# SiLU and tanh as single table functions in a fused two-block transformer kernel, with a shorter routing step

## What is computed

```python
# first block
c_act = silu(causal_conv(c, conv_w, conv_b))
h = head_layernorm(mlstm(...), m_norm_g) + m_skip * c_act
y_m = sigmoid(z) * h
y_d = rmsnorm(diff_attention(qd, kd, vd, lam, rel_bias), da_norm_g) * (1 - lam_init)
x = x + concat([y_m, y_d]) @ w_out
lg = h2 @ w_rg + b_rg                       # 4 groups; best group by top_k
le = (h2 @ w_re + b_re)[best group]         # 8 experts; best two by top_k
gates = one_hot(eid) * (pg_sel * softmax(top_v))
for e in range(32):                         # 32 experts, hidden 512
    hid = silu(t @ w_eg[e]) * (t @ w_eu[e])
    out = out + gates[:, e:e+1] * (hid @ w_ed[e])
# second block, two layers
x = x + 0.5 * rmsnorm((silu(a) * b) @ w_out)       # a, b = split(rmsnorm(x) @ w_in); width 2816
xbc = silu(causal_dwconv(xbc));  y_ssd = rmsnorm(ssd(xbc, dt) * silu(z))
y_ret = groupnorm(retention(q, k, v)) * silu(g)
y_att = sliding window attention with sinks
y = sum over branches of sigmoid(gate + b_gate) * (y_branch @ w_branch);  x = x + rmsnorm(y @ w_out)
x = x + 0.5 * rmsnorm(feed-forward again)
```

## Time and profile before

| what | before |
|---|---|
| median of 3 runs | 2215.17 us (2214.47 to 2215.31) |
| the profiled execution's own time | 2214.65 us |
| its span, first to last instruction | 2212.8 us |
| PE busy | 2024.2 us (91%) |
| DVE busy | 1154.8 us (52%) |
| ACT busy | 1096.2 us (50%) |
| mean granted clock of PE, of full speed | 0.937 |
| moved by DMA | 486 MB, 220 GB/s on average |

### The profile page before, as it was taken

One profiled execution on the slowest core, in us unless ns is written; L12 is line 12 of the kernel. 1 busy time (PEld: TensorE's weight loads), 2 busy tenths in 40 slices (PEclk: granted clock), 3 DMA queues, 4 the chain that ended last, 5 costly groups with the idle time before them and its releaser, 6 DMA issues.

```text
span 2212.8 us, 31344 instructions
## 1 busy us (share of the span) xinstructions
PE 2024.2 (91%) x13110; PEld 1639.5 (74%) x13110; DVE 1154.8 (52%) x1468; ACT 1096.2 (50%) x1368; POOL 50.2 (2%) x99
## 2 busy tenths in 40 slices
PE   8978677777789999999999999999999999999998
PEld 7863212111269978987799999899879888898997
DVE  5763111111146656647566565465575565655663
ACT  5520000000068934553555897498544635646992
POOL 0000000000000000000000000000000000001000
PEclk9988877777789999999999999999999999999999
DMA  6558999999974554432344555535545233354552
GB/s 270 212 225 334 421 421 421 421 421 421 421 304 151 213 189 173 170 114 96 114 172 172 191 177 188 181 134 229 190 171 189 97 115 123 127 189 174 181 182 94
DMA packets 66904, 486.14 MB, mean 220 GB/s; under 512 B 7424, under 2 KB 7424, under 8 KB 8544
## 3 DMA queue, kind: packets, MB, share of 16 engines
q1 hardware_dynamic: 65632, 476.25, 56.3%
q0 software_dynamic: 1152, 8.16, 1.0%
HBM read 483.33 MB, written 1.05 MB: 219 GB/s over the span
## 4 chain that ended last, share of the span: by engine, by line
PE 77%; DMA 10%; SPq 6%; DVE 3%; ACT 2%; issue 1%; POOL 1%; DVEq 0%; ACTq 0%; POOLq 0%
PE bank L1534 35%; PE bank L1621 11%; PE bank L456 10%; DMA work<-in_w_experts 9%; PE bank L1837 8%; SPq L1434 6%; PE bank L1548 3%; PE bank L1362 1%; PE bank L1392 1%; PE bank L1415 1%; PE bank L1078 1%; PE bank L2067 1%; ACT rows L2222 1%; PE bank L1937 1%; PE bank L1964 0%
## 5 line engine op out<-in xcount | busy, mean ns | idle before, releaser
L1534 PE MATMUL bank<-work_parts 128*128 128x256 f32 x2240 | 581.2, 283 | 0.0
L1512 DVE TENSOR_TENSOR ring_parts<-ring,work_parts 128x2048 fp32r<-128x2048 f32 x200 | 457.6, 2291 | 232.3 <-ACT work_parts L1505 219.7
L1505 ACT ACTIVATE work_parts<-ring 128x2048 fp32r<-128x2048 f32 x200 | 380.8, 1908 | 202.5 <-PE bank L1621 98.3
L1534 PE MATMUL bank<-columns_parts,work_parts 128*128 128x256 f32 x1472 | 417.9, 284 | 2.1 <-DVE rows_parts L680 1.9
L1534 PE MATMUL bank<-columns_parts,ring_parts 128*128 128x256 f32 x1472 | 416.8, 283 | 0.0
L1534 PEld LDWEIGHTS bank<-work_parts 128*128 128x128 f32 x2240 | 411.6, 192 | 0.1
L1534 PEld LDWEIGHTS bank<-columns_parts,work_parts 128*128 128x128 f32 x1472 | 282.8, 192 | 3.1 <-DVE ring_parts L669 2.3
L1534 PEld LDWEIGHTS bank<-columns_parts,ring_parts 128*128 128x128 f32 x1472 | 282.5, 192 | 0.0
L1621 PE MATMUL bank<-work_parts 128*128 128x512 f32 x704 | 217.3, 389 | 0.0
L1392 PE MATMUL bank<-work 128*32 128x512 f32 x640 | 126.7, 888 | 60.6 <-DMA work<-in_w_experts 60.6
L1534 PE MATMUL bank<-rows_parts,work_parts 128*128 128x256 f32 x640 | 181.7, 284 | 0.0
(11 more groups left out here) (388 smaller groups left out, 2776.4 us busy)
## 6 DMA issues: line engine op xcount, KB each, us to landing
ring<-in_w_layers SPq DMA_DIRECT2D x242, 1024.0 KB, 4.8
work<-in_w_experts SPq DMA_DIRECT2D x136, 1024.0 KB, 26.9
ring<-in_w_experts SPq DMA_DIRECT2D x48, 1024.0 KB, 26.7
ring<-in_w_first SPq DMA_DIRECT2D x16, 1024.0 KB, 4.9
columns<-in_w_experts SPq DMA_DIRECT2D x8, 1024.0 KB, 26.6
work<-in_post POOLq DMA_DIRECT2D x3, 1024.0 KB, 5.5
work<-in_second POOLq DMA_DIRECT2D x1, 2944.0 KB, 11.4
work<-in_first SPq DMA_DIRECT2D x1, 1805.5 KB, 11.2
```

The lines of the kernel that those rows point to most:

```text
L1505: act.activation(his[j % len(his)], m.ring[U.slot(names[j])], ACT.Copy).then_inc(F["unit_hi"], 1)
L1512: dve.tensor_tensor(m.ring_r[slot], m.ring[slot], his[j % len(his)].bitcast(F32), ALU.subtract).then_inc(F["unit_lo"], 1)
L1534: mm = pe.matmul(out, w, x, start=k + n == 0, stop=k == KT - 1 and n == 2)
```

## The change

It replaces Exp, Ln, Exp and a multiplication by one Silu wherever SiLU is wanted: the convolutions of both blocks, the experts' gate, the feed-forward, rg and z of the mixer. Where a sigmoid is wanted (the first block's gate, the branch gates), it uses sigmoid(x) = (1 + tanh(x/2)) / 2. ACT takes tanh from the bank, DVE does (t + 1) * y in one instruction, and the factor 1/2 goes into the step that makes the high and the low part. In the first block z.1 is projected before h is turned, and DVE does the normalisation of the attention half before the skip and the gate. The routing chain loses a few small operations: the two token halves go together, the subtraction of the two best logits moves behind `chosen`, and before the first selection only the first pass's ranks are made. SP's order of loads follows. The diff, cut:

```diff
-              + [f"vdtok.{t}" for t in range(2)] + ["z.0", "dout.0", "dout.1", "hT.0", "hT.1", "z.1", "ydT.0", "ydT.1"]
+              + [f"vdtok.{t}" for t in range(2)] + ["z.0", "dout.0", "dout.1", "z.1", "hT.0", "hT.1", "ydT.0", "ydT.1"]
...
@@ first_scalar
     act.wait_ge(*F.at("conv", 4))
-    step(act.activation(m.ec, m.cv, ACT.Exp, scale=-1.0))
-    sigmoid_tail(act, step, m.ec, F["conv_sig"])
+    act.activation(m.cv, m.cv, ACT.Silu).then_inc(F["cact"], 1)
...
-        act.activation(m.ez[:, 2 * i:2 * i + 2, :], split(ps[B.bank(job)][:], 2), ACT.Exp, scale=-1.0).then_inc(B.free(job), 1)
+        act.activation(m.ez[:, 2 * i:2 * i + 2, :], split(ps[B.bank(job)][:], 2), ACT.Tanh, scale=0.5).then_inc(B.free(job), 1)
...
     act.activation(m.dsq, m.yd, ACT.Square).then_inc(F["d_sq"], 1)
+    gate(1)
     first_unit("out.1.0")
-    gate(1)
     act.wait_ge(*F.at("ym", 1))
-    whole(slice(0, 2))
+    whole(slice(0, 2), 0.5)
+    act.wait_ge(*F.at("ym", 2))
+    whole(slice(2, 4), 0.5)
     first_unit("out.0.1")
...
@@ first_vector
-    dve.wait_ge(*F.at("conv_sig"))
-    dve.tensor_tensor(m.cv, m.cv, m.ec, ALU.mult).then_inc(F["cact"], 1)
...
-        step(dve.tensor_scalar(e, e, 1.0, None, ALU.add))
-        step(dve.reciprocal(e, e))
...
-        dve.tensor_tensor(m.yT[:, c, :], m.yT[:, c, :], m.ez[:, c, :], ALU.mult).then_inc(F["ym"], 1)
+        dve.wait_ge(*B.drained(f"z.{i}"))
+        dve.scalar_tensor_tensor(out=m.yT[:, c, :], in0=m.ez[:, c, :], scalar=1.0, in1=m.yT[:, c, :], op0=ALU.add,
+                                 op1=ALU.mult).then_inc(F["ym"], 1)
...
-    gate(0)
     dve.wait_ge(*F.at("d_sq"))
     dve.tensor_reduce(m.dv, m.dsqh, AX.X, ALU.add).then_inc(F["d_var"], 1)
-    skipped(0)
-    skipped(1)
     dve.wait_ge(*F.at("d_rstd"))
     dve.tensor_tensor(m.ydh, m.ydh, bc(m.dv, [P, 8, P]), ALU.mult).then_inc(F["dn"], 1)
+    skipped(0)
+    gated(0)
+    skipped(1)
+    low(0, slice(0, 2), 0.5)
     first_unit("out.1.0")
-    gated(0)
-    low(0, slice(0, 2))
-    gate(1)
     gated(1)
-    low(1, slice(2, 4))
+    low(1, slice(2, 4), 0.5)
...
@@ first_tensor
+    project("z.1")
     turn_heads("hT", m.hm, "hn")
-    project("z.1")
     turn_heads("ydT", m.ydh, "dn")
...
@@ route_vector
-    for t in range(TT):
-        step(dve.tensor_tensor(r.by_group[:, t], r.lg[:, t, 4:36].rearrange("p (g j) -> p g j", g=GROUPS),
-                               bc(r.group[:, t, :], [P, GROUPS, PER_GROUP]), ALU.mult))
-        step(dve.tensor_reduce(r.le[:, t, :], r.by_group[:, t].rearrange("p g j -> p j g"), AX.X, ALU.add))
-    step(dve.tensor_scalar(r.e2, r.best, -1.0, None, ALU.mult))
+    step(dve.tensor_tensor(r.by_group, by_group(r.lg[:, :, 4:36]), bc(r.group, full), ALU.mult))
+    step(dve.tensor_reduce(r.le, r.by_group.rearrange("p t g j -> p t j g"), AX.X, ALU.add))
...
-    for t in range(TT):
-        ins = dve.tensor_tensor(r.ranks[:, t, 0:PASSES * EXPERTS].rearrange("p (q e) -> p q e", q=PASSES),
-                                r.rank[:, t, :].unsqueeze(1).to_broadcast([P, PASSES, EXPERTS]),
-                                bc(m.c["first"], [P, PASSES, EXPERTS]), ALU.subtract)
+    step(dve.tensor_scalar(r.ranks[:, :, 0:EXPERTS], r.rank, m.c["first"][:, 0:1], None, ALU.subtract))
     moe_select(dve, m, m.sel, 0).then_inc(sel_ready, 1)
+    for t in range(TT):
+        ins = dve.tensor_tensor(r.ranks[:, t, EXPERTS:PASSES * EXPERTS].rearrange("p (q e) -> p q e", q=PASSES - 1),
+                                r.rank[:, t, :].unsqueeze(1).to_broadcast([P, PASSES - 1, EXPERTS]),
+                                bc(m.c["first"][:, 1:], [P, PASSES - 1, EXPERTS]), ALU.subtract)
+    step(ins)
...
@@ moe_vector, moe_scalar
-        dve.tensor_scalar(m.eg, m.eg, 1.0, None, ALU.add).then_inc(M["dve_step"], 1)
-        dve.reciprocal(m.eg, m.eg).then_inc(M["dve_step"], 1)
-        dve.tensor_tensor(m.eg, m.eg, ps[GATE][:], ALU.mult).then_inc(M["dve_step"], 1)
-        act.activation(m.eg, ps[GATE][:], ACT.Exp, scale=-1.0).then_inc(M["gate_exp"], 1)
+        act.activation(m.eg, ps[GATE][:], ACT.Silu).then_inc(M["gate_silu"], 1)
...
@@ moe_loads
     load_after("z.0")
+    sp.wait_ge(*F.at("d_var"))
+    load(13, 0)
+    load_after("z.1")
     sp.wait_ge(*B.filled("hT.1"))
     load(14, 0)
-    load_after("z.1")
-    sp.wait_ge(*F.at("d_var"))
-    load(13, 0)
...
@@ ffn_scalar, ffn_vector
-        step(act.activation(e, ps[B.bank(job)][:, 0:T], ACT.Exp, scale=-1.0))
-        step(act.activation(e, e, ACT.Ln, bias=1.0))
-        act.activation(e, e, ACT.Exp, scale=-1.0).then_inc(F["ffn_exp"], 1)
+        act.activation(e, ps[B.bank(job)][:, 0:T], ACT.Silu).then_inc(F["ffn_silu"], 1)
-        step(dve.tensor_tensor(e, e, bank[:, 0:T], ALU.mult))
...
@@ mix_scalar, mix_vector
-        ins = act.activation(m.zT[:, 2 * i:2 * i + 2, :], split(ps[B.bank(job)][:], 2), ACT.Exp, scale=-1.0)
-        if i % 2:
-            step(ins)
-            sigmoid_tail(act, step, m.zT[:, 2 * i - 2:2 * i + 2, :], F["z_sig"])
+        act.activation(m.zT[:, 2 * i:2 * i + 2, :], split(ps[B.bank(job)][:], 2), ACT.Silu).then_inc(B.free(job), 1)
...
-            ins = act.activation(gates_of(m, i)[:, k, :], ps[B.bank(job)][:, k * T:(k + 1) * T], ACT.Exp,
-                                 bias=m.nbg[:, n:n + 1], scale=-1.0)
+            ins = act.activation(gates_of(m, i)[:, k, :], ps[B.bank(job)][:, k * T:(k + 1) * T], ACT.Tanh,
+                                 bias=m.hbg[:, n:n + 1], scale=0.5)
```

More of the change, by code:

```diff
@@ L491, in load_units @@
             after_first()
-def sigmoid_tail(act, step, e, flag):
-    step(act.activation(e, e, ACT.Ln, bias=1.0))
-    act.activation(e, e, ACT.Exp, scale=-1.0).then_inc(flag, 1)
 def first_scalar(act, step, m, ps, B, U, F):
@@ L854, in first_vector @@
     first_unit("out.0.1")
-    low(2, slice(4, 8))
+    low(2, slice(4, 8), 1.0)
     first_unit("out.1.1")
@@ L1153, in route_tensor, with first_of @@
     pe.matmul(bank[:, 64:96], ones, chosen[:, 1, :], start=False, stop=True).then_inc(B.full("rank"), 1)
-def first_of(dve, step, values, best, prior, out):
+def first_of(dve, step, values, best, prior, out, top):
     n = values.shape[2]
@@ L1181, in route_vector, with by_group @@
-    step(dve.tensor_reduce(r.best, r.le, AX.X, ALU.max))
-    step(dve.tensor_scalar(r.e2, r.best, -1.0, None, ALU.mult))
-    first_of(dve, step, r.le, r.best, m.c["prior8"], r.hot1)
+    step(dve.tensor_reduce(r.best1, r.lg[:, :, 0:4], AX.X, ALU.max))
+    dve.tensor_scalar(r.nmg, r.best1, -1.0, None, ALU.mult).then_inc(F["lg_max"], 1)
+    first_of(dve, step, r.lg[:, :, 0:4], r.best1, m.c["prior4"], r.group, r.best)
+    full = [P, TT, GROUPS, PER_GROUP]
+    def by_group(rows):
+        return rows.rearrange("p t (g j) -> p t g j", g=GROUPS)
@@ L1194, in route_vector @@
-    ins.then_inc(F["chosen"], 1)
+    dve.tensor_tensor(by_group(r.chosen), bc(r.group, full), r.le.unsqueeze(2).to_broadcast(full),
+                      ALU.mult).then_inc(F["chosen"], 1)
+    dve.tensor_tensor(r.e2, r.best2, r.best1, ALU.subtract).then_inc(F["le_diff"], 1)
     step(dve.memset(r.ranks[:, :, PASSES * EXPERTS:], -1.0))
+    dve.wait_ge(*F.at("chosen"))
     dve.wait_ge(*B.filled("rank"))
@@ L2123, in mix_scalar @@
             act.wait_ge(*B.filled(job))
-            ins = act.activation(m.rg[:, t, n * 512:(n + 1) * 512], ps[B.bank(job)][:], ACT.Exp, scale=-1.0)
-    step(ins)
+            act.activation(m.rg[:, t, n * 512:(n + 1) * 512], ps[B.bank(job)][:], ACT.Silu).then_inc(B.free(job), 1)
     for i in range(6):
@@ L2130, in mix_scalar @@
         act.activation(m.xpad[:, 2 * i:2 * i + 2, 3:], split(ps[B.bank(job)][:], 2), ACT.Copy).then_inc(B.free(job), 1)
-        if i == 0:
-            step(act.activation(m.rg, m.rg, ACT.Ln, bias=1.0))
-        elif i == 1:
-            act.activation(m.rg, m.rg, ACT.Exp, scale=-1.0).then_inc(F["rg_sig"], 1)
     for name, n in (("rqT", 0), ("rkT", 1)):
@@ L2141, in mix_scalar @@
                            ACT.Copy).then_inc(B.free(job), 1)
-    for i, (lo, hi) in enumerate(CONV_PARTS):
+    for lo, hi in CONV_PARTS:
         act.wait_ge(*F.at("conv", hi))
-        if i:
-            act.wait_ge(*F.at("xc", i))
-        e = m.ce[:, 0:hi - lo, :]
-        step(act.activation(e, m.xc[:, lo:hi, :], ACT.Exp, scale=-1.0))
-        sigmoid_tail(act, step, e, F["conv_sig"])
+        act.activation(m.xc[:, lo:hi, :], m.xc[:, lo:hi, :], ACT.Silu).then_inc(F["xc"], 1)
     act.activation(m.acol[0:16, 0:1], lp["alog"][0:16, :], ACT.Exp).then_inc(F["a"], 1)
@@ L2239, in mix_scalar @@
     gate(0, 3)
-    for i in range(4):
-        act.wait_ge(*B.drained(f"g.0.{i}"))
-    sigmoid_tail(act, step, m.sg, F["gate_sig"])
     for t in range(TT):
@@ L2266, in mix_scalar @@
             gate(b, i)
-        for i in range(4):
-            act.wait_ge(*B.drained(f"g.{b}.{i}"))
-        end_unit(u + 4)
-        step(act.activation(m.sg, m.sg, ACT.Ln, bias=1.0))
-        end_unit(u + 5)
```

(9 more changed lines are left out.)

111 lines of the change are left out of this document (42 added, 69 removed).

## The result

| what | before | after |
|---|---|---|
| median | 2214.82 us (2214.07 to 2215.31, 4 runs) | 2195.41 us (2194.24 to 2197.72, 4 runs) |
| span of the profiled execution | 2212.8 us | 2192.5 us |
| PE busy | 2024.2 us | 2010.1 us |
| DVE busy | 1154.8 us | 1056.5 us |
| ACT busy | 1096.2 us | 727.6 us |

The ratio is 0.9909, with a 95% interval of 0.9896 to 0.9923: 19.4 us faster by the medians, where 12.4 were forecast.

What follows compares the result with a forecast made beforehand. PE was taken to bound the kernel outside the experts; gains of 5.0 (first block), 1.3 (routing), 3.4 (z pauses) and 2.7 (clock) sum to 12.4, so 2214.65 - 12.4 = 2202.3 us, range 2197.5 to 2209.5.

Steps and rivals of the forecast that it cites:

- What bounds the kernel: Whole program: PE, 91% busy, sets the pace; outside the experts an edit pays only where PE stands still.
- The rival in which ACT paces the feed-forward: Feed-forward, 88 units: ACT's 5.68 us holds PE at 5.76, so Silu gains 4.4 us, 2197.9; chance 0.01.
- First block, 5.0 us: First block, gate and turns: PE starts the output projection near 119.1 instead of 124.16, a gain of 5.0 us.
- the replay: First block: step-by-step timing of the engines with the edits, ending with the output projection's start at 119.1 us.
- Routing, 1.3 us: Routing: 0.8 us less before PE's ranks and 0.5 after them, 1.3 in all, bounds 0.9 to 1.5.
- Experts at nothing, the stream moved by 6.3 us: Experts: no gain inside a turn; the DMA stream's start and end move forward by 5.0 + 1.3 = 6.3 us.
- Near 171 us: Sign at the experts: their DMA stream starts near 171 us instead of 177, still at 419 GB/s.
- z pauses, 3.4 us: Both mixers: z's banks are given back earlier, so PE's two 1.7 us waits at the B/C scores go, 3.4 us.
- No wait takes their place: Answers a mixer rival: the 1.7 us return at the transposes behind the B/C scores, total 2208.3; chance 0.09.
- Clock, "Without the pause I expect no fall: 2.7 us more": Second layer's mixer: the fall to half clock behind the B/C-score pause goes with the pause, 2.7 us more.
- The rival that priced the clock: Second block: moved pauses lower the mean clock from 0.98 to 0.97, 15.7 us slower, 2218.0; chance 0.04.
- The remaining pauses: Mixers: PE's 3.3 us pause at the attention scores stays in both layers.

Runs made afterwards that it cites:

- the second profile: The changed kernel once more, unedited, run for another profile: 2196.15 us (2193.05 to 2197.66).
- filling the pause: The kernel before, with four more B/C-score matmuls keeping PE at work in the z pause, results overwritten: 2213.06 us, ratio 1.0003.
- the early gate: The changed kernel with branch gate g.0.1 read after 5 of the 16 exponentials of the attention scores instead of after all: 2187.19 us, ratio 0.9873.
- two reorderings of one step each: The changed kernel with g.0.1 read after 5 of 16 exponentials and one DVE low part moved behind the second turn's copies of the probabilities: 2180.32 us, ratio 0.9837.

## Why the prediction was wrong

- *What bounds the kernel*: right. Outside the experts only PE's pauses counted; 286 us less of ACT work measured 2214.98 us against 2214.51. The rival in which ACT paces the feed-forward is out. By the drain that the Trainium skill gives for a table switch ("ScalarE: Activation LUTs", What ACT_TABLE_LOAD costs) it would have been worth an estimated 236 us: no run here shows any of that.
- *First block, 5.0 us*: right. Alone the replay came out at 119.11 for 119.1, to the tenth by luck, and 4.2 us by the medians. In the changed kernel's own profile the projection starts at 122.10: z.0's projection began 2.0 us later there than in the kernel with the first block's edits alone (101.87 for 99.86 us) and ran its first 19 matmuls at half clock, the 7.80 us of the chain above.
- *Routing, 1.3 us*: right. PE's two waits went from 6.9 and 1.8 us to 6.2 and 1.3, 1.2 in all.
- *Experts at nothing, the stream moved by 6.3 us*: right in mechanism, 419 GB/s before and after; first block, routing and experts together measured 6.3 by the medians and 7.3 by the starts of the second block. "Near 171 us" came out between 176 and 177 and, in the second profile, between 171 and 172: one profile could not carry that sign.
- *z pauses, 3.4 us*: the mechanism is right and the size was short. No wait takes their place, and at full clock they are worth 2.23 us each, 4.5.
- *Clock, "Without the pause I expect no fall: 2.7 us more"*: this is the step that failed. The stretch right behind the pause cost what I gave it: filling the pause brought 2.66 us back. But the sum took every other fall as fixed, without a reason, and so put the clock of all other stretches at nothing. With the z edit alone, three stretches without any edit lost 1.18 + 1.64 + 2.95 = 5.8 us of half clock. With 4.5 for the pauses and 2.6 for the half clock behind one that is 12.9 us, less 0.2 that the other stretches took longer: 12.6 us, by which the second block of that profile is shorter (1570.7 for 1583.3), beside 12.1 by the medians. The forecast had 3.4 + 2.7 = 6.1.
- *The rival that priced the clock* had the size, 0.01 of mean clock or 15.7 us, and only one sign. I gave it a place on the slow side and let the low end of the range have 0.002 of it. With that much either way the range would have begun near 2187 (2202.3 - 15.7).
- *The remaining pauses*: right. 3.3 us at the attention scores in both layers, until the early gate took them away.

What stays open is why those three stretches ran at a better clock. The z pause's idle time is not the cause for the two attentions, since filling it left them no better; the last feed-forward got 1.3 of its 2.95 us by it. The relieved ACT and DVE are not the cause, since neither the feed-forward alone nor the mixer without z showed it. A move of the whole block makes single stretches shorter, with z's pause still there: both attentions in the kernel with first block, routing and experts. But there other stretches became longer by as much, and the block that lay 6.2 us earlier did not change at all. What is left is that the work behind each z comes 2.2 us earlier against the work ahead of it. That is an inference from what was excluded; no run shows it. And the seven executions of the kernel before at 2203.1 to 2205.5 us show that it can lose as much with its pauses in place; where in the kernel, no profile tells.

The Trainium skill calls the clock's monitor free-running ("TensorE: Matmul & The Clock Gate", Part 1). The two profiles of the changed kernel agree: one stretch of the same instructions and pauses took 53.21 us in one and 54.86 in the other. It is not a new draw each time, though: layer 1's attention took 56.08 us in the kernel before and in that with the first block's edits alone, and 56.09 with the feed-forward's alone.

## What to carry to other kernels

On an engine that sets the pace, count its pauses, not the work beside it: z's banks given back earlier were worth 12 us here by the medians, and 286 us of ACT work nothing. Where pauses can be followed by half clock, price a removed pause at its length plus what follows it, and widen the range by the half clock of all other pauses, on both sides: here it changed in stretches that nobody had edited. Look at how the executions of the kernel before are spread, too: here seven of 86 lay apart, as far away as the gain in question. Look for the next pauses with the same eye: two reorderings of one step each gave another 15 us, nearly as much as the whole change.
